# One layer of a streaming encoder: the slots of the split-weight ring get a pitch of 1032 elements

## The chip, the cores and the metric

The kernel runs on one core of one Trainium2 chip. The metric is the time of one execution in microseconds (us), as the median of three runs. The profile is of one further execution, and its times are also in us unless marked ns.

## The reference, cut to what matters

One layer takes `x` (256 tokens by 2048 channels, float32) through a token-mixing half and a feed-forward half:

```python
h = rmsnorm(x, g_pre_mix)
proj = h @ w_in                       # 2048 x (8 groups of 2048 + 16 gates + 2048)
...                                   # mLSTM heads and differential attention on proj
y_m = (sigmoid(m_o) * hm) @ w_branch_m
y_a = ha @ w_branch_a
mix = (g_m * y_m + g_a * y_a) @ w_out
x = x + rmsnorm(mix, g_post_mix)
h = rmsnorm(x, g_pre_ffn)
u = causal_dwconv(h @ w_up)           # 2048 x 11264
y = (gelu(gate) * val) @ w_down       # 5632 x 2048
x = x + rmsnorm(y, g_post_ffn)
```

Nearly all the arithmetic is in the products of a 256-row activation with large float32 weights, and every weight is read from memory once.

## The kernel before

**Split products.** Each float32 operand is split into two float32r parts, `hi` (the rounded value) and `lo` (the rest). A product is then three matmuls into one place in PSUM: hi times hi, hi times lo, lo times hi. The helper `three` (lines 1110 to 1114) issues them in the order of lines 1112, 1113, 1114: stationary hi with moving hi, stationary hi with moving lo, stationary lo with moving hi. Each matmul loads its stationary operand anew.

**The ring of weights.** Weights pass in 648 units of 1024 columns (`UNIT`), 512 KB each, through a ring of `RING = 4` slots. For unit n, SyncE loads `raw[slot]` by DMA; ScalarE writes `w_hi[slot]` as a rounded copy of it (line 517, in `split`); VectorE writes `w_lo[slot] = raw - w_hi` (line 813); TensorE then runs the unit's matmuls and gives the slot back. The splits run three units ahead (`LOOKAHEAD`).

**Stages on TensorE.**
- Gates: 48 matmuls with a small piece of `w_in`, kept in `hm_hi` and `hm_lo`, as the stationary operand and `h` as the moving one.
- Mixer, 4 turns of 64 units. In 6 of 8 chunks the weight is stationary and `h_hi` or `h_lo` is moving (`unit_channels`: 24 matmuls of 256 columns in a unit). In the other 2 chunks `h` is stationary and the weight moves (`unit_tokens`: 12 matmuls of 512 columns). The heads' small matmuls stand between the units.
- Branches, 4 turns of 24 units, all `unit_channels`: 8 units with `h`, 8 with `hm_hi`/`hm_lo`, 8 with `ha_hi`/`ha_lo` as the moving operand.
- Output projection and down projection, 32 and 88 units of `rows_unit` (lines 1278 to 1292): a tile of activations `ks_hi`/`ks_lo` is stationary, the weight moves, 12 matmuls of 512 columns in a unit. The last four units of each use `h_hi` and `h_lo` as room for their split weights.
- Up projection, 176 units of `unit_channels` with `h` moving.

So there are 9600 matmuls with the weight stationary and `h` moving, 1536 with the weight stationary and `hm` or `ha` moving, 768 with `h` stationary, and 1440 in the two row stages.

**What sets the order.** Nothing is scheduled by a program. Every engine runs its own list in the order written, and semaphores tie the lists together.

**Where the tensors lie.** SBUF tensors are laid one behind another in each partition, in the order of the `sb(...)` calls, each start rounded up to 32 bytes: `raw`, `w_hi`, `w_lo`, `h_hi`, `h_lo`, `chan`, `shp`, `stat`, `terms`, `gm`, `hm_hi`, `hm_lo`, `ha_hi`, `ha_lo`, then the heads' tensors; `ks_hi` and `ks_lo` stand further on. `h`, `hm` and `ha` are 16 tiles of 1024 bytes, a slot is 4096 bytes, and each of a slot's stationary tiles of 128 columns is 512 bytes. The built program has these start addresses in a partition, in bytes:

| tensor | before | before, modulo 512 |
|---|---|---|
| `raw` | 16512 | 128 |
| `w_hi` | 32896 | 128 in every slot |
| `w_lo` | 49280 | 128 in every slot |
| `h_hi`, `h_lo` | 65664, 82048 | 128 |
| `hm_hi`, `hm_lo`, `ha_hi`, `ha_lo` | 119872, 136256, 152640, 169024 | 64 |
| `ks_hi`, `ks_lo` | 209984, 214080 | 64 |

Of the kernel before, what the change touches and what calls it, by code (L numbers as in the profile page):

```python
# [40 lines left out]
F32R = mybir.dt.float32r  # L41
# [5 lines left out]
P = 128  # L47
# [20 lines left out]

RING = 4
UNIT = 1024  # L70
LOOKAHEAD = 3
UNITS_CHUNK = KT // 2
TURNS_MIX, U_MIX = 4, 8 * UNITS_CHUNK
# [55 lines left out]
def build_layer(nc, x, w_in, w_branch_m, w_branch_a, w_out, g_post_mix, w_up, w_down, g_post_ffn,  # L129
# [9 lines left out]
    with ctx:  # L139
        def sb(name, shape, dt=F32, stack=ctx):  # L140
            return stack.enter_context(nc.sbuf_tensor(name, shape, dt))
# [3 lines left out]


        raw = sb("raw", [P, RING, UNIT])
        w_hi = sb("w_hi", [P, RING, UNIT], F32R)
        w_lo = sb("w_lo", [P, RING, UNIT], F32R)
        h_hi = sb("h_hi", [P, KT, T], F32R)  # L150
        h_lo = sb("h_lo", [P, KT, T], F32R)
        chan = sb("chan", [P, C_ALL])
# [158 lines left out]

        h_units = [part[:].rearrange("p k t -> p (k t)").rearrange("p (s c) -> p s c", c=UNIT) for part in (h_hi, h_lo)]

# [38 lines left out]
        def _(sp):  # L352
            def load(n, slot, dst_src):
                sp.wait_ge(raw_free, n + 1)
                dst, src = dst_src
                sp.dma_start(dst, src).then_inc(raw_loaded[slot], 16)
# [6 lines left out]
            def rows_loads(turns, per_turn, base, view):  # L363
                for u in range(per_turn):
                    k, half = rows_place(u, True)
                    load(base + u, u % RING, (raw[:, u % RING:u % RING + 1, :],
                                              view[:, k:k + 1, half * UNIT:(half + 1) * UNIT]))
                with sp.Fori(1, turns - 1) as turn:
                    for u in range(per_turn):
                        k, half = rows_place(u, False)  # L370
                        load(turn * per_turn + (base + u), u % RING,
                             (raw[:, u % RING:u % RING + 1, :],
                              view[:, ds(turn * 4 + k, 1), half * UNIT:(half + 1) * UNIT]))
                for u in range(per_turn):
# [140 lines left out]
        def _(scalar):  # L515
# [3 lines left out]
            def split(n4, n, slot):  # L519

                scalar.wait_ge(raw_loaded[slot], n4 * 16 + 16)
                scalar.wait_ge(pe_done, n + 1)
                copy(w_hi[:, slot, :], raw[:, slot, :]).then_inc(hi_done, 1)

            def split_ahead(turn, per_turn, base, u):
                u += LOOKAHEAD
                split(turn * (per_turn // RING) + (base + u) // RING, turn * per_turn + (base + u), u % RING)
# [5 lines left out]
            def norm_tiles(count, gain):  # L533

                for k in range(KT):
                    if k % 2 == 0:
                        scalar.wait_ge(h_psum, (count + k) // 2 + 1)
                    ins = copy(h_hi[:, k, :], ps[:, tile_bank(k), k % 2 * T:k % 2 * T + T],
                               scale=chan[:, gain + k:gain + k + 1])
                    if k % 2:  # L540
                        ins.then_inc(h_hi_done, 1)
# [27 lines left out]
            norm_tiles(0, C_GPM)  # L569
            for u in range(1, LOOKAHEAD):  # L570
                split(0, u, u)
# [117 lines left out]
            def split_last(first_unit, u):  # L689
                n = first_unit + u  # L690
                scalar.wait_ge(raw_loaded[u % RING], n // RING * 16 + 16)
                if u < RING:
                    scalar.wait_ge(pe_done, n + 1)
                copy(last_split(u)[0], raw[:, u % RING, :]).then_inc(hi_done, 1)

            def rows_phase(turns, per_turn, base, src, scale, src_ready, then_load, rest=None):
# [6 lines left out]
                def turn(g, first, last):  # L703
                    for u in range(per_turn):
                        if not last:
                            split_ahead(g, per_turn, base, u)
                        elif u + LOOKAHEAD < per_turn:
                            split_last(g * per_turn + base, u + LOOKAHEAD)
                        if first and u == 5:
# [97 lines left out]
        def _(vec):  # L807
# [3 lines left out]
            def split(n, slot):  # L811
                vec.wait_ge(hi_done, n + 1)
                nc.vector.tensor_tensor(w_lo[:, slot, :], raw[:, slot, :], w_hi[:, slot, :].bitcast(F32),  # L813
                                        ALU.subtract).then_inc(lo_done, 1)

            def split_ahead(turn, per_turn, base, u):
                u += LOOKAHEAD
                split(turn * per_turn + (base + u), u % RING)

            def norm_tiles(count, gain, halfway=None):  # L820
                for k in range(KT):
                    if k == KT // 2 and halfway:
                        halfway()
                    if k % 2 == 0:
                        vec.wait_ge(h_hi_done, (count + k) // 2 + 1)
                    stt(h_lo[:, k, :], ps[:, tile_bank(k), k % 2 * T:k % 2 * T + T], chan[:, gain + k:gain + k + 1],
                        h_hi[:, k, :].bitcast(F32), ALU.mult, ALU.subtract).then_inc(h_done, 1)
# [25 lines left out]
            norm_tiles(0, C_GPM)  # L853
            for u in range(1, LOOKAHEAD):
                split(u, u)
# [518 lines left out]
```

## Time and profile before

| | |
|---|---|
| median of 3 runs | 1934.59 us (1934.44 to 1935.26) |
| the profiled execution's own time | 1934.15 us |
| its span, first to last instruction | 1932.4 us |
| TensorE matmul busy | 1901.5 us, 98% of the span |
| VectorE, ScalarE busy | 1099.8 us (57%), 897.5 us (46%) |
| DMA | 351.35 MB, mean 182 GB/s |

A group's "mean ns of one" for a matmul is its whole pass through the array. Neighbouring matmuls overlap in it, so it is longer than the distance between two starts. What one more matmul costs is that distance, which a list of instructions in order of time shows. TensorE is busy in nearly the whole span, and the granted clock is full in nearly all of it, so the time is close to the sum of these distances.

### The profile page before, as it was taken

To read this page: it belongs to the slowest core of one execution; us is meant where nothing else is said; L and a number is where in the kernel's file an instruction comes from. 1 tells how busy PE (TensorE), PEld (TensorE's weight loads), DVE (VectorE), ACT (ScalarE), POOL (GpSimd) and SP (SyncE) were. 2 spreads that over 40 slices of the span, in tenths; PEclk is the share of its full clock that TensorE was granted. 3 is DMA by queue.
4 is the path that set the end of the run, shared out by engine and by line. 5 is a ranking of instruction groups with operands and counts; after the bars stand their busy time and mean duration, and the time that the engine had idled before them with its cause. 6 is when DMAs were issued, how large, how long until landed. Compare 5 with 4: busy or idle time off the path is not lost.

```text
span 1932.4 us, 35840 instructions
## 1 busy us (share of the span) xinstructions
PE 1901.5 (98%) x13774; PEld 1805.6 (93%) x13774; DVE 1099.8 (57%) x1287; ACT 897.5 (46%) x1159; POOL 74.9 (4%) x103
## 2 busy tenths in 40 slices
PE   6999999999999999999999998999999999999998
PEld 6999999999999999999999888999999999988886
DVE  5555555645655466444554556666666666755545
ACT  5444445444544455443434455454444554544443
POOL 4600000000000000000000000000000000000000
PEclk9999999999999999999999998999999999999999
DMA  6655655566555655565665754666666666565554
GB/s 206 197 174 165 181 172 172 174 175 175 170 179 170 177 166 180 170 191 190 185 191 190 256 177 142 182 183 181 183 184 183 179 182 183 182 214 190 192 189 141
DMA packets 166294, 351.35 MB, mean 182 GB/s; under 512 B 12916, under 2 KB 13517, under 8 KB 165581
## 3 DMA queue, kind: packets, MB, share of 16 engines
q1 hardware_dynamic: 165005, 344.40, 58.5%
q10 hardware_dynamic: 848, 4.79, 0.6%
q0 software_dynamic: 368, 1.09, 0.2%
q8 instruction: 58, 0.95, 0.2%
q14 instruction: 15, 0.12, 0.0%
HBM read 348.12 MB, written 2.12 MB: 181 GB/s over the span
## 4 chain that ended last, share of the span: by engine, by line
issue 59%; PE 39%; SPq 0%; POOLq 0%; DVE 0%; DMA 0%; ACT 0%; POOL 0%; DVEq 0%; ACTq 0%
PE ps L1112 12%; PE ps L1114 12%; PE ps L1113 12%; PE ps L1174 1%; PE ps L1247 1%; PE ps L1224 0%; PE ps L1182 0%; DMA raw<-in_w_in 0%; POOLq L446 0%; PE ps L1223 0%; SPq L387 0%; POOL stat L447 0%; SPq L389 0%; PE ps L1230 0%; SPq L381 0%
## 5 line engine op out<-in xcount | busy, mean ns | idle before, releaser
L813 DVE TENSOR_TENSOR w_lo<-raw,w_hi 128x1024 fp32r<-128x1024 f32 x638 | 781.9, 1229 | 721.4 <-ACT w_hi L517 718.3
L517 ACT ACTIVATE w_hi<-raw 128x1024 fp32r<-128x1024 f32 x640 | 676.3, 1059 | 841.7 <-PE ps L1114 681.8
L1112 PE MATMUL ps<-h_hi,w_hi 128*128 128x256 f32 x3200 | 908.3, 284 | 0.0
L1114 PE MATMUL ps<-h_hi,w_lo 128*128 128x256 f32 x3200 | 905.7, 283 | 0.0
L1113 PE MATMUL ps<-h_lo,w_hi 128*128 128x256 f32 x3200 | 905.7, 283 | 0.0
L1112 PEld LDWEIGHTS ps<-h_hi,w_hi 128*128 128x128 f32 x3200 | 614.5, 192 | 0.5
L1113 PEld LDWEIGHTS ps<-h_lo,w_hi 128*128 128x128 f32 x3200 | 614.5, 192 | 0.5
L1114 PEld LDWEIGHTS ps<-h_hi,w_lo 128*128 128x128 f32 x3200 | 614.3, 192 | 0.0
L1286 PE MATMUL ps<-w_hi,ks_hi 128*128 128x512 f32 x448 | 176.0, 393 | 0.2 <-DVE ks_lo L809 0.2
L1290 PE MATMUL ps<-w_lo,ks_hi 128*128 128x512 f32 x448 | 175.1, 391 | 0.0
L1286 PE MATMUL ps<-w_hi,ks_lo 128*128 128x512 f32 x448 | 138.7, 391 | 0.0
L1286 PEld LDWEIGHTS ps<-w_hi,ks_lo 128*128 128x128 f32 x448 | 84.1, 188 | 19.0
L1286 PEld LDWEIGHTS ps<-w_hi,ks_hi 128*128 128x128 f32 x448 | 84.2, 188 | 18.5 <-issue 0.4
L1290 PEld LDWEIGHTS ps<-w_lo,ks_hi 128*128 128x128 f32 x448 | 84.1, 188 | 18.1
L1112 PE MATMUL ps<-w_hi,h_hi 128*128 128x512 f32 x256 | 100.9, 394 | 0.0
L1113 PE MATMUL ps<-w_lo,h_hi 128*128 128x512 f32 x256 | 99.7, 390 | 0.0
L1114 PE MATMUL ps<-w_hi,h_lo 128*128 128x512 f32 x256 | 99.7, 389 | 0.0
L809 DVE SCALAR_TENSOR_TENSOR xn<-ps,chan,xn 128x254 f32<-128x254 f32 (+1 forms) x176 | 76.6, 477 | 28.4 <-ACT xn L767 21.3
L1112 PE MATMUL ps<-hm_hi,w_hi 128*128 128x256 f32 x256 | 70.7, 276 | 0.0
L1113 PE MATMUL ps<-hm_lo,w_hi 128*128 128x256 f32 x256 | 70.7, 276 | 0.0
L1114 PE MATMUL ps<-hm_hi,w_lo 128*128 128x256 f32 x256 | 70.7, 276 | 0.0
L1112 PE MATMUL ps<-ha_hi,w_hi 128*128 128x256 f32 x256 | 70.7, 276 | 0.0
(166 smaller groups left out, 1381.0 us busy)
## 6 DMA issues: line engine op xcount, KB each, us to landing
raw<-in_w_in SPq DMA_DIRECT2D x288, 512.0 KB, 3.7
raw<-in_w_up SPq DMA_DIRECT2D x176, 512.0 KB, 4.1
raw<-in_w_down SPq DMA_DIRECT2D x88, 512.0 KB, 4.6
raw<-in_w_branch_m SPq DMA_DIRECT2D x32, 512.0 KB, 4.7
raw<-in_w_branch_a SPq DMA_DIRECT2D x32, 512.0 KB, 4.6
raw<-in_w_out SPq DMA_DIRECT2D x32, 512.0 KB, 3.8
x<-in_x ACTq DMA_DIRECT2D x1, 2048.0 KB, 11.6
gm<-in_x SPq DMA_DIRECT2D x3, 512.0 KB, 6.5
```

The lines of the kernel that those rows point to most:

```text
L517: return nc.scalar.activation(out_ap, in_ap, ACT.Copy, scale=scale)
L809: return nc.vector.scalar_tensor_tensor(out=out_ap, in0=in0, scalar=scalar, in1=in1, op0=op0, op1=op1)
L813: nc.vector.tensor_tensor(w_lo[:, slot, :], raw[:, slot, :], w_hi[:, slot, :].bitcast(F32), ALU.subtract).then_inc(lo_done, 1)
L1112: nc.tensor.matmul(out_ap, stat_hi, mov_hi, start=start, stop=False, skip_group_check=True)
L1113: nc.tensor.matmul(out_ap, stat_hi, mov_lo, start=False, stop=False, skip_group_check=True)
L1114: return nc.tensor.matmul(out_ap, stat_lo, mov_hi, start=False, stop=stop, skip_group_check=True)
L1174: last = nc.tensor.matmul(out_ap, weights[:, part * P:(part + 1) * P], v[:, s, j, 0:out_ap.shape[1]], start=i == 0, stop=i == len(parts) - 1)
L1247: last = nc.tensor.matmul(ps[:, 4 + j, (0, 256)[s]:(256, 384)[s]], kT[:, 2 * j + dt, s * P:(s + 1) * P], qT[:, 2 * j + dt, s * P:T], start ...
L1286: ins = nc.tensor.matmul(o, a, hi[:, n * 512:n * 512 + 512], start=first and kslot == 0 and part is ks_hi, stop=last and kslot == 3 and pa ...
L1290: nc.tensor.matmul(o, a, lo[:, n * 512:n * 512 + 512], start=False, stop=False, skip_group_check=True)
```

## The change

`w_hi` and `w_lo` get rows of 1032 elements for each slot, of which the first 1024 are used; a slot is now 4128 bytes behind the one before it. A small unused tensor `w_rest` follows them. Its size works out as 64 elements (256 bytes), so that `h_hi` starts at a whole multiple of 512 bytes behind `w_hi`.

```diff
 RING = 4
 UNIT = 1024
+PITCH = UNIT + 8
 LOOKAHEAD = 3
...
         raw = sb("raw", [P, RING, UNIT])
-        w_hi = sb("w_hi", [P, RING, UNIT], F32R)
-        w_lo = sb("w_lo", [P, RING, UNIT], F32R)
+        w_hi = sb("w_hi", [P, RING, PITCH], F32R)[:, :, 0:UNIT]
+        w_lo = sb("w_lo", [P, RING, PITCH], F32R)[:, :, 0:UNIT]
+        sb("w_rest", [P, 2 * (UNIT - RING * (PITCH - UNIT) % UNIT) % P])
         h_hi = sb("h_hi", [P, KT, T], F32R)
         h_lo = sb("h_lo", [P, KT, T], F32R)
```

Every engine's list of instructions, with their order, shapes and waits, stays the same. Only start addresses change. With s as the slot (0 to 3), they are:

| tensor | after | after, modulo 512 |
|---|---|---|
| `raw` | 16512 | 128 |
| `w_hi` slot s | 32896 + 4128 s | 128 + 32 s |
| `w_lo` slot s | 49408 + 4128 s | 256 + 32 s |
| `h_hi`, `h_lo` | 66176, 82560 | 128 |
| `hm_hi`, `hm_lo`, `ha_hi`, `ha_lo` | 120384, 136768, 153152, 169536 | 64 |
| `ks_hi`, `ks_lo` | 210496, 214592 | 64 |

Everything behind `w_lo` moves by 512 bytes, so it keeps its start modulo 512; the slots of `w_hi` and `w_lo` do not.

## Rows read from the trace of the kernel before

**Rows 1.** The page: busy time of TensorE; its granted clock in 40 slices.

```profile
PE 1901.5 (98%) x13774; PEld 1805.6 (93%) x13774; DVE 1099.8 (57%) x1287; ACT 897.5 (46%) x1159; POOL 74.9 (4%) x103
...
PEclk9999999999999999999999998999999999999999
```

**Rows 2.** Waits of TensorE: total us, times, longest.

```profile
PE ps L1191 <- DMA prob<-in_channel_rows: 13.6, 1, 13.6
PE ps L1148 <- DVE xn L837: 7.8, 1, 7.8
PE ps L1148 <- DVE h_lo L809: 0.8, 1, 0.8
PE ps L1286 <- DVE ks_lo L809: 0.2, 1, 0.2
```

**Rows 3.** Groups by line and shape: count, busy us, mean ns, idle before.

```profile
L1112 PE MATMUL ps<-h_hi,w_hi 128*128 128x256 f32 x3200 | 908.3, 284 | 0.0
...
L1112 PE MATMUL ps<-hm_hi,w_hi 128*128 128x256 f32 x256 | 70.7, 276 | 0.0
...
L1112 PE MATMUL ps<-ha_hi,w_hi 128*128 128x256 f32 x256 | 70.7, 276 | 0.0
```

**Rows 4.** Two stretches of one branch turn: busy us (instructions), granted clock, DMA.

```profile
876.00:894.00 18.00, 18.00 (x152) 18.00 (x151) 7.99 (x7) 7.07 (x7) 0.00 (x0) 1.00 0.56 179
898.00:916.00 18.00, 18.00 (x162) 18.00 (x161) 8.54 (x7) 7.44 (x7) 0.00 (x0) 1.00 0.59 191
```

**Rows 5.** TensorE in order of time, `h` moving: start us, duration us.

```profile
874.80 0.28 PE L1112 MATMUL ps<-h_hi,w_hi 128*128 128x256 f32 x1
...
881.40 0.28 PE L1113 MATMUL ps<-h_lo,w_hi 128*128 128x256 f32 x1
```

**Rows 6.** The same view, `hm` moving.

```profile
899.78 0.28 PE L1112 MATMUL ps<-hm_hi,w_hi 128*128 128x256 f32 x1
...
906.47 0.28 PE L1114 MATMUL ps<-hm_hi,w_lo 128*128 128x256 f32 x1
```

**Rows 7.** The same view, the gates: `hm` stationary, `h` moving.

```profile
21.87 0.28 PE L1113 MATMUL ps<-h_lo,hm_hi 128*128 128x256 f32 x1
...
27.29 0.28 PE L1114 MATMUL ps<-h_hi,hm_lo 128*128 128x256 f32 x1
```

**Rows 8.** The same view, `unit_tokens`: `h` stationary, the weight moving.

```profile
153.55 0.39 PE L1112 MATMUL ps<-w_hi,h_hi 128*128 128x512 f32 x1
...
162.85 0.39 PE L1114 MATMUL ps<-w_hi,h_lo 128*128 128x512 f32 x1
```

**Rows 9.** The same view, down projection: `ks` stationary, the weight moving.

```profile
1705.02 0.39 PE L1290 MATMUL ps<-w_lo,ks_hi 128*128 128x512 f32 x1
...
1715.78 0.39 PE L1286 MATMUL ps<-w_hi,ks_hi 128*128 128x512 f32 x1
```

**Rows 10.** All engines in order of time: matmuls and loads of stationary operands (PEld).

```profile
299.82 0.28 PE L1113 MATMUL ps<-h_lo,w_hi 128*128 128x256 f32 x1
299.82 0.19 PEld L1114 LDWEIGHTS ps<-h_hi,w_lo 128*128 128x128 f32 x1
299.94 0.28 PE L1114 MATMUL ps<-h_hi,w_lo 128*128 128x256 f32 x1
299.94 0.19 PEld L1112 LDWEIGHTS ps<-h_hi,w_hi 128*128 128x128 f32 x1
```

**Rows 11.** The page: the splits on VectorE and ScalarE, as Rows 3.

```profile
L813 DVE TENSOR_TENSOR w_lo<-raw,w_hi 128x1024 fp32r<-128x1024 f32 x638 | 781.9, 1229 | 721.4 <-ACT w_hi L517 718.3
L517 ACT ACTIVATE w_hi<-raw 128x1024 fp32r<-128x1024 f32 x640 | 676.3, 1059 | 841.7 <-PE ps L1114 681.8
```

## The prediction

> **What bounds the kernel now.** I read the page first. TensorE is busy in 98% of the span, and the granted clock reads full (2.4 GHz) in nearly every slice [rows 1]. Next, the waits of TensorE: 13.6, 7.8, 0.8 and 0.2 us [rows 2], all of them at the start or between the two halves. So no buffer, DMA or other engine sets the pace. What sets it is the distance between the starts of two matmuls, taken 13774 times.
>
> Then the groups. The same instruction has a mean of 284 ns with `h` moving and 276 ns with `hm` or `ha` moving [rows 3]. It has the same shape, line and stationary tensor. Two stretches of 18 us inside one branch turn show the same: 152 matmuls with `h`, 162 with `hm`, both at clock 1.00 [rows 4]. For exact distances I divide the time between two far starts by the matmuls between them:
> - `h` moving: 6.60 us over 55 matmuls, 120.0 ns [rows 5].
> - `hm` moving: 6.69 us over 59, 113.4 ns [rows 6].
> - gates, `hm` stationary and `h` moving: 5.42 us over 46, 117.8 ns [rows 7].
> - `unit_tokens`: 9.30 us over 41, 226.8 ns for 512 columns [rows 8].
> - down projection: 10.76 us over 47, 228.9 ns for 512 columns [rows 9].
>
> From 256 to 512 columns at the same distance of operands, 120.0 becomes 226.8 ns, so 256 further columns cost 106.8 ns. That is what 256 columns take at one per cycle of 2.4 GHz (106.7 ns). So 106.7 is the floor of a 256-column matmul, and 120.0 holds 13.3 ns of something else.
>
> What else differs between the first three? Only addresses. The load of the next stationary operand starts with each matmul [rows 10], so two streams read SBUF together: the moving operand of one matmul and the stationary operand of the next. Let d be the stationary start minus the moving start, modulo 512 bytes. Before, d is 0 for the weights against `h` (128 - 128) in every slot, +64 against `hm` and `ha` (128 - 64), and -64 in the gates and the row stages (64 - 128). My reading is that d sets the extra time: 120.0 at 0, 113.4 at +64, 117.8 at -64. Higher address bits seem not to matter. The 9600 `h` matmuls take every slot, every k tile and both odd and even multiples of 512, and rows 3 show one mean for them. The 284 ns there fits the 120.0 ns of rows 5.
>
> This bears on a rule. The Trainium skill's page "TensorE: Matmul & The Clock Gate", section "Step-by-step: what each phase is for", says TensorE has two independent SBUF read ports, and that loading the next weights takes no read bandwidth from the running matmul. "SBUF — State Buffer", section "Who interferes with whom", adds that PE never waits on anyone. By that rule no address could matter and the change would be worth 0. The 120.0 against 113.4 ns of rows 5 and 6 speaks against it; the rule has a rival below.
>
> **The change part by part.** It removes and adds no instruction and moves none in its queue. After it, by the start addresses:
> - Weights against `h`: `w_hi` slot s has d = 32s, which is 0, 32, 64, 96; `w_lo` has d = 128 + 32s, which is 128, 160, 192, 224. In each triple two loads are of `w_hi` and one of `w_lo`, so of the 9600 matmuls each slot has 1600 of the first kind and 800 of the second.
> - Against `hm` and `ha` (1536): `w_hi` 64, 96, 128, 160; `w_lo` 192, 224, 256, 288.
>
> Two classes are known from rows. Slot 0 of `w_hi` keeps d = 0: 1600 matmuls stay at 120.0, worth nothing. Slot 2 of `w_hi` gets d = 64, today's distance of `hm`: 1600 x (113.4 - 120.0) = -10.6 us.
>
> The other 6400 `h` matmuls have distances that no row shows. Bounds: the floor 106.7 from below. From above, the highest extra seen is that of rows 9, 228.9 less 106.7 for the second 256 columns, which is 122.2 ns. I take 117.1, the mean of the three levels seen (120.0, 113.4, 117.8), since no row is nearer to any of these distances than the others. That is 6400 x -2.9 = -18.6 us (bounds -85.1 and +14.1).
>
> The branches: of the 1536, the 256 with `w_hi` in slot 0 (two thirds of a quarter) keep d = 64. The other 1280 go from 113.4 to 117.1: +4.7 us (bounds -8.6 and +11.3).
>
> `unit_tokens` (768) and the row stages (1440): the weight is now the moving operand, and d changes in all but slot 0 of `w_hi`. Rows 8 and 9 show only 226.8 and 228.9 for two different d, so long matmuls look less sensitive. I take 0. Bounds: down to twice the floor, 213.4, which is 768 x 13.4 + 1440 x 15.5, some -33 us; and up by the 2.1 ns between these rows, +5 us.
>
> The splits: VectorE and ScalarE now write slots at other offsets, off the critical path either way. A channel unit on TensorE is 24 x 120.0 = 2.88 us, against 1.23 and 1.06 us for its two splits, and VectorE idles 718.3 us waiting for ScalarE, which idles 681.8 us waiting for TensorE [rows 11]. At 24 x 113.4 = 2.72 us a unit they stay hidden. `raw` doesn't move, so the DMAs are the same. The 512 bytes by which all other tensors move leave their starts modulo 512 as they are. The float32 matmuls of the heads have no `w` in them: 0.
>
> Sum: -10.6 - 18.6 + 4.7 + 0 = -24.5 us. On the profiled execution's 1934.15 us (span 1932.4 and 1.75 around it) that is 1909.7, and the median is 0.44 above that execution, so 1910 us. The gain can't be given back by a wait: nothing else is near TensorE's pace.
>
> **The rivals.**
> *The unknown distances are nearly free.* Then 6400 matmuls sit between the floor and 113.4, say at 110.0: -64.0 - 10.6 - 1280 x 3.4 = -79 us, 1856 us. For it: d = 0 looks like the most crowded case, with both streams at the same offset, and a move by 64 took half of the extra away. Against: -64 took away only 2.2 of 13.3 ns, so a move alone doesn't free it.
>
> *The distance isn't what counts.* Either the two reads don't meet at all, or the moving operand's own start decides (`hm` starts at 64 modulo 128, `h` at 128, before and after). Both give 0: 1934.6 us. The first is what the two pages of the Trainium skill named above say. For the second: it explains rows 5 against 6. Against: the gates move the same `h` as the branches and take 117.8 instead of 120.0 [rows 5, 7], with only the stationary operand's place changed.
>
> *The unknown distances are worse.* A larger distance could make the two streams meet more often, not less: within a matmul they sweep 1024 and 512 bytes, so d only says where they begin. The place is every channel unit, slots 1 and 3 and all `w_lo`. At the upper bound of 122.2 ns the cost is 6400 x 2.2 = +14.1, and the branches, which stand at the best level known, lose 1280 x 8.8 = +11.3; with -10.6 that is +15 us, 1949 us. It decides when the mean of the unknown distances passes 120.2 ns: there -10.6 + 6400 x 0.2 + 1280 x 6.8 is about 0. For it: the long matmuls at -64 are slower than at 0 [rows 8, 9]. Against: of three short levels none is above 120.0.
>
> **How the numbers follow.** Forecast 0.60, nearly free 0.13, no effect 0.11, worse 0.16. A change within 0.2% (3.9 us) can't be told from none. So faster 0.73, same 0.11, slower 0.16. The forecast's own range is 1885 to 1928, the unknown mean level between 114 and 119.5 with a few us for the long matmuls. For 8 in 10 I reach down to 1868, which leaves out most of the nearly free case, and up to 1944, which takes in no effect and the milder half of worse.
>
> **What the profile after would show.** By slot, channel units of `h`: slot 2's `w_hi` intervals at 113.4, slot 0's at 120.0, and the two must differ between slots that before were alike. If slot 2 stays at 120.0, the distance modulo 512 is the wrong variable. The `hm` and `ha` stretches should lose their even 113.4. TensorE's waits should stay at 22 us and the clock full; a new wait of TensorE for `w_lo` would make the covered splits wrong. If the mean over the 6400 is outside 114 to 119.5, the step that failed is the value taken for the unknown distances.

## The result, and the profile after

| | before | after |
|---|---|---|
| median of 4 runs on one chip | 1934.92 us | 1924.64 us |
| ratio | | 0.9947, 95% interval 0.9934 to 0.9959 |
| span of the profiled execution | 1932.4 us | 1922.5 us |

The change makes the kernel 10 us faster. The direction and the place were right; the size forecast, -24.5 us, was 2.4 times the measured one.

Lines of the changed kernel are two higher than before (1112 is 1114). These are its groups by line and shape: count, busy us, mean ns, idle before. They answer to [rows 3].

```profile
L1114 PE MATMUL ps<-h_hi,w_hi 128*128 128x256 f32 x3200 | 899.7, 281 | 0.0
...
L1288 PE MATMUL ps<-w_hi,ks_hi 128*128 128x512 f32 x448 | 176.3, 394 | 0.0
...
L1114 PE MATMUL ps<-w_hi,h_hi 128*128 128x512 f32 x256 | 101.9, 398 | 0.0
...
L1115 PE MATMUL ps<-hm_lo,w_hi 128*128 128x256 f32 x256 | 71.9, 281 | 0.0
```

The mean with `h` moving fell from 284 to 281 ns and the one with `hm` rose from 276 to 281 (line 1115; its line before, 1113, stood at 276 as well). The waits of TensorE (us in total, times, longest) are what they were, but for one at the start that grew from 0.8 to 2.1 us in this execution; the one of 0.2 us is gone:

```profile
PE ps L1193 <- DMA prob<-in_channel_rows: 13.6, 1, 13.6
PE ps L1150 <- DVE xn L839: 7.8, 1, 7.8
PE ps L1150 <- DVE h_lo L811: 2.1, 1, 2.1
```

Two stretches of the changed kernel, inside `h` and inside `hm` units of one branch turn. As in [rows 4], a line has the stretch and its length, then the busy us and the instructions (x) of TensorE's matmuls, of its loads, of VectorE, ScalarE and GpSimd, then the granted clock, the DMA share and GB/s:

```profile
876.00:894.00 18.00, 18.00 (x156) 18.00 (x155) 7.36 (x7) 8.34 (x8) 0.00 (x0) 1.00 0.58 187
898.00:914.00 16.00, 16.00 (x138) 16.00 (x137) 7.27 (x7) 6.37 (x6) 0.00 (x0) 1.00 0.60 188
```

With `h`, 18 us now hold 156 matmuls instead of 152. With `hm`, 16 us hold 138; the old rate of 113.4 ns puts 143 there (141, and the two that reach over the edges).

The long matmuls became slower too. The same 40 us of the down projection, before and after, hold 177 and 175:

```profile
1690.00:1730.00 40.00, 40.00 (x177) 32.81 (x176) 21.74 (x24) 18.04 (x23) 0.00 (x0) 1.00 0.66 220
1690.00:1730.00 40.00, 40.00 (x175) 32.49 (x174) 19.98 (x23) 18.37 (x23) 0.00 (x0) 1.00 0.59 202
```

I took the distance between neighbouring starts for every matmul of both traces and summed it by kind (differences are taken before rounding):

| kind | before, us | after, us | difference | predicted |
|---|---|---|---|---|
| 9600 with `h` moving | 1154.9 | 1130.5 | -24.4 | -29.2 |
| 1536 with `hm` or `ha` moving | 174.5 | 181.1 | +6.6 | +4.7 |
| 768 of `unit_tokens` | 175.7 | 179.0 | +3.4 | 0 |
| 1440 of the row stages | 329.9 | 333.0 | +3.0 | 0 |
| all else | 97.3 | 98.9 | +1.5 | 0 |
| span | 1932.4 | 1922.5 | -9.9 | -24.5 |

By slot, in the up projection, where 176 units run without a break, 44 of each slot:

| slot | distance of `w_hi`, `w_lo` from `h` | before, ns | after, ns |
|---|---|---|---|
| 0 | 0, 128 | 120.0 | 119.3 |
| 1 | 32, 160 | 120.0 | 117.9 |
| 2 | 64, 192 | 120.0 | 114.8 |
| 3 | 96, 224 | 120.1 | 117.8 |

So the distance from start to start does depend on where the weights lie. The writes of the splits into the same memory are not what it depends on. In the up projection before, the mean distance is 120.0 ns for the matmuls during which VectorE was writing a `w_lo` (some 1600) and 120.0 for the others (some 2600); after, it is 117.4 and 117.5.

### The profile page after: what moved, and what is told of

Same layout as the page of the kernel before. It is cut to its first block, busy times and chain, and to the rows that moved or that the text cites. A ratio compares the mean times of both kernels' runs of the same rounds, so it can differ in the third digit from the quotient of the medians.

```text
span 1922.5 us, 35840 instructions
## 1 busy us (share of the span) xinstructions
PE 1890.7 (98%) x13774; PEld 1788.4 (93%) x13774; DVE 1099.3 (57%) x1287; ACT 898.7 (47%) x1159; POOL 75.4 (4%) x103
## 4 chain that ended last, share of the span: by engine, by line
issue 59%; PE 39%; SPq 0%; POOLq 0%; DMA 0%; DVE 0%; ACT 0%; POOL 0%; DVEq 0%; ACTq 0%
PE ps L1116 12%; PE ps L1114 12%; PE ps L1115 12%; PE ps L1176 1%; PE ps L1249 1%; PE ps L1226 0%; PE ps L1184 0%; DMA raw<-in_w_in 0%; POOLq L448 0%; PE ps L1225 0%; SPq L389 0%; POOL stat L449 0%; PE ps L1150 0%; PE ps L1232 0%; SPq L383 0%
## 5 line engine op out<-in xcount | busy, mean ns | idle before, releaser
L1115 PE MATMUL ps<-h_lo,w_hi 128*128 128x256 f32 x3200 | 896.3, 280 | 0.0
L1116 PE MATMUL ps<-h_hi,w_lo 128*128 128x256 f32 x3200 | 895.2, 280 | 0.0
L1115 PEld LDWEIGHTS ps<-h_lo,w_hi 128*128 128x128 f32 x3200 | 603.9, 189 | 0.6
L1116 PEld LDWEIGHTS ps<-h_hi,w_lo 128*128 128x128 f32 x3200 | 602.9, 188 | 0.0
L1114 PEld LDWEIGHTS ps<-h_hi,w_hi 128*128 128x128 f32 x3200 | 602.2, 188 | 0.6
L1115 PE MATMUL ps<-ha_lo,w_hi 128*128 128x256 f32 x256 | 71.9, 281 | 0.0
L1116 PE MATMUL ps<-ha_hi,w_lo 128*128 128x256 f32 x256 | 71.8, 280 | 0.0
```

The costliest lines, as they stand in the source:

```text
L1114: nc.tensor.matmul(out_ap, stat_hi, mov_hi, start=start, stop=False, skip_group_check=True)
L1115: nc.tensor.matmul(out_ap, stat_hi, mov_lo, start=False, stop=False, skip_group_check=True)
L1116: return nc.tensor.matmul(out_ap, stat_lo, mov_hi, start=False, stop=stop, skip_group_check=True)
```

## The experiments

The padded kernels below add unused SBUF only; all do the same arithmetic. "Distance" is stationary start minus moving start modulo 512 bytes, as in the prediction. The times of e3, e4, e10 and e11 are single runs.

### e1_d64 and e8_d64_again: all weights at 64

```diff
+        sb("pad_h", [P, 112])
         h_hi = sb("h_hi", [P, KT, T], F32R)
         h_lo = sb("h_lo", [P, KT, T], F32R)
+        sb("pad_chan", [P, 16])
         chan = sb("chan", [P, C_ALL])
```

> Before, with 448 unused bytes ahead of h_hi and 64 behind h_lo: every weight tile stands at +64 modulo 512 from h, hm and ha; nothing else changes modulo 512. Distance theory (stationary start minus moving start, modulo 512, sets the extra time): all 9600 matmuls with h moving take 113.4 ns instead of 120.0, -63 us; unit_tokens goes from distance 0 to -64 and so from 226.8 to about 229, +2 us; 1874 us. The gates go from -64 to 0, 117.8 to 120.0. Rival 'no contention': 1935 us. Rival 'the moving operand's own start modulo 128': h now starts at 64 as hm does, so it also gives 113.4; the next kernel tells these two apart.

Measured: 1894.77 us, ratio 0.9791 (0.9775 to 0.9807). That is 20 us short of the theory, and one of the five runs took 1912.69 us. The mean with `h` moving was 117.2 ns in its trace, and `hm` and `ha`, whose distance I hadn't touched, had gone from 113.4 to 117.8. One distance, two levels: so the prediction's premise, one level for each distance, fell here. The same kernel again:

> The kernel with h, hm and ha all at 64, once more. Its five runs were 1893.96, 1894.60, 1894.77, 1894.84 and 1912.69 us, and the last is the one profiled, with its 4224 matmuls of the up projection at 117.7 ns. Theory of two levels: 4224 x 4.4 ns = 18.6 us is the whole gap, so the other runs had 113.3 in the up projection; the times of this kernel fall into separate clusters about 19 us apart (or sums of such steps for the other stages), none in between. A profile of a run near 1894 would show the up projection at 113.3 ns. Rival (some other disturbance in one run): all runs near 1894, and their profile has 117.7 in the up projection just the same.

Measured: 1893.98, 1894.07, 1895.05, 1895.86, 1895.99 and 1913.08 us. Two clusters again, and this time the profiled run was one near 1894. The same stretch of the up projection in both executions, first the one of 1912.69 us:

```profile
1200.00:1240.00 40.00, 40.00 (x342) 40.00 (x342) 25.77 (x32) 19.78 (x24) 0.00 (x0) 1.00 0.61 182
1400.00:1440.00 40.00, 40.00 (x342) 40.00 (x342) 26.47 (x31) 20.45 (x24) 0.00 (x0) 1.00 0.64 187
```

and the one of 1894.07 us:

```profile
1200.00:1240.00 40.00, 40.00 (x355) 40.00 (x355) 27.44 (x34) 19.64 (x24) 0.00 (x0) 1.00 0.61 193
1400.00:1440.00 40.00, 40.00 (x356) 40.00 (x355) 28.18 (x35) 21.27 (x25) 0.00 (x0) 1.00 0.59 188
```

The program and the granted clock (1.00) are the same, yet 40 us hold 342 matmuls or 355. A stretch also counts the two or three that reach over its edges; without them it is 117.8 and 113.3 ns. Once in a level the stream stays in it for all 176 units; in the mixer the level changes only where the heads' small matmuls or long matmuls come between. 4224 x 4.5 ns = 19 us is the gap between the clusters. (One execution of each cluster was profiled.)

Two smaller predictions of e1 held, in both traces: the gates, now at 0, went from 117.8 to 120.0 ns, and `unit_tokens`, now at -64, took 1.5 us more (+2 expected).

### e2_all_moved: every tensor 64 bytes further on

```diff
+        sb("pad_raw", [P, 16])
         raw = sb("raw", [P, RING, UNIT])
```

> Before, with 64 unused bytes ahead of raw: every tensor starts 64 bytes further on, all distances between them are the same. Distance theory: every interval as before (120.0 with h moving, 113.4 with hm), 1935 us. Rival 'the moving operand's own start modulo 128 decides': h now starts at 64 modulo 128 and hm at 0, so h falls to 113.4 and hm rises to 120.0: 9600 x -6.6 + 1536 x 6.6 = -53 us, 1882 us.

Measured: 1934.86 us, ratio 1.0002 (0.9993 to 1.0012). The stretch that answers to the first of [rows 4]:

```profile
876.00:894.00 18.00, 18.00 (x152) 18.00 (x152) 9.46 (x9) 6.50 (x7) 0.00 (x0) 1.00 0.62 188
```

The same 152. A shift of everything by 64 bytes changes nothing, so the rival of the moving operand's own start is out: what counts is relative.

### e5_pitch_only and e6_lo128_only: the two parts of the change apart

```diff
-        w_hi = sb("w_hi", [P, RING, UNIT], F32R)
-        w_lo = sb("w_lo", [P, RING, UNIT], F32R)
+        w_hi = sb("w_hi", [P, RING, PITCH], F32R)[:, :, 0:UNIT]
+        sb("pad_lo", [P, 96])
+        w_lo = sb("w_lo", [P, RING, PITCH], F32R)[:, :, 0:UNIT]
+        sb("pad_h", [P, 96])
```

> The change without the 128-byte offset of w_lo: slots of w_hi and w_lo both stand at 0, 32, 64, 96 from h. Levels of the changed kernel by slot are 119.6, 118.0, 114.8, 117.9 ns. If the pitch makes the change's time, this kernel has the same levels and 1923 to 1927 us. Rival: the offset of w_lo (128) makes it, then this one is near 1935.

```diff
         w_hi = sb("w_hi", [P, RING, UNIT], F32R)
+        sb("pad_lo", [P, 32])
         w_lo = sb("w_lo", [P, RING, UNIT], F32R)
+        sb("pad_h", [P, 96])
```

> The change without the pitch: all slots of w_hi at 0 from h, all of w_lo at 128; against hm 64 and 192. If the pitch makes the change's time, h stays at the 119.6 ns of the changed kernel's slot 0 and hm near 114: 1930 to 1936 us. Rival (w_lo's offset makes it): 1923 to 1927 us.

Measured: pitch alone 1933.72 us, ratio 0.9998 (0.9989 to 1.0007); offset alone 1933.35 us, 0.9995 (0.9986 to 1.0004). Neither is a measurable gain, and together they give 10 us. I had expected the pitch to carry it; that was wrong. By slot in the up projection, pitch alone has 119.9, 118.2, 117.9 and 117.4 ns, offset alone 119.1 in all. What pitch alone lacks is slot 2, 117.9 instead of 114.8. Its -16.2 us on `h` are eaten by +7.4 us on `hm` and `ha`, +3.4 us on `unit_tokens` and +5.0 us on the row stages. Offset alone leaves `hm` and `ha` (here at 64 and 192) at 113.3, but its -8.5 us on `h` are eaten by +6.6 us on the long matmuls. On `h` the two gains simply add up (-24.7, against -24.4 together). What makes the whole worth more than its parts is the losses: each part alone pays for the long matmuls (+8.4 and +6.6), and both together pay once (+6.4).

Pitch alone also shows 64 with 64 in two ways of coming in. In its up projection slot 2, behind slot 1 at 32, stays at 117.9 in all 44 units. In its branches slot 0 has the same 64 with 64, behind slot 3 at 96 or 160, and falls to 113.3 after some four matmuls in all 16 units.

### e12_slot2_lo64: one address of the changed kernel

The slots are cut by hand from one long row; the offsets in elements are those of the changed kernel except slot 2 of `w_lo` (and a place for slot 3 that has the same start modulo 512).

```diff
+HI_OFF = (0, 8, 16, 24)
+LO_OFF = (0, 8, 112, 152)
...
+        w_hi = Ring(sb("w_hi", [P, RING * UNIT + 32], F32R), HI_OFF)
+        w_lo = Ring(sb("w_lo", [P, RING * UNIT + 152], F32R), LO_OFF)
+        sb("pad_h", [P, 72])
```

> The changed kernel with one address changed modulo 512: w_lo of slot 2 at 64 from h instead of 192 (and at 128 instead of 256 from hm and ha). Theory: slot 2 no longer gets to 113.3 and goes from 114.8 to 118, 2400 x 3.0 = +7 us over the changed kernel, 1930 to 1933 us. Rival (slot 2 is fast because w_hi is at 64): slot 2 stays near 115, 1923 to 1926 us.

Measured: 1931.15 us, ratio 0.9981 (0.9972 to 0.9991). Slot 2 is at 118.0 ns, the others at 118.9, 117.9 and 117.9. A slot 2 unit of the changed kernel, with its 24 matmuls from 1281.29 on, in order of time (start, duration):

```profile
1281.29 0.28 PE L1114 MATMUL ps<-h_hi,w_hi 128*128 128x256 f32 x1
...
1282.00 0.28 PE L1114 MATMUL ps<-h_hi,w_hi 128*128 128x256 f32 x1
...
1283.93 0.28 PE L1116 MATMUL ps<-h_hi,w_lo 128*128 128x256 f32 x1
```

The same unit with `w_lo` at 64:

```profile
1284.37 0.28 PE L1125 MATMUL ps<-h_hi,w_hi 128*128 128x256 f32 x1
...
1285.08 0.28 PE L1125 MATMUL ps<-h_hi,w_hi 128*128 128x256 f32 x1
...
1287.08 0.28 PE L1127 MATMUL ps<-h_hi,w_lo 128*128 128x256 f32 x1
```

Both begin with 0.71 us for six matmuls, 118 ns each. Then the changed kernel takes 1.93 us for 17, 113.5 each; with the one address moved it is 2.00 us, 117.6 each. So slot 2 of the changed kernel isn't fast because `w_hi` is at 64 alone, but because `w_hi` at 64 together with `w_lo` at 192 pulls the stream into the low level within six matmuls. Once there, the loads of `w_hi` and of `w_lo` cost the same: all three lines stand at 113.4.

### e9_hi64_lo192: that pair in every slot

```diff
         w_hi = sb("w_hi", [P, RING, UNIT], F32R)
+        sb("pad_lo", [P, 32])
         w_lo = sb("w_lo", [P, RING, UNIT], F32R)
+        sb("pad_h", [P, 80])
         h_hi = sb("h_hi", [P, KT, T], F32R)
         h_lo = sb("h_lo", [P, KT, T], F32R)
+        sb("pad_chan", [P, 16])
```

> In the changed kernel slot 2 has w_hi at 64 and w_lo at 192 from h, and falls to 113.3 ns within its first 6 matmuls even out of slot 1's 118; with both at 64 (pitch alone) slot 2 stays at 118. Theory: the pair 64/192 has only the low level, or pulls the stream to it; the pair 64/64 holds either. Here all slots have 64/192 against h, hm and ha. Theory: 113.3 in every channel stage of every run: 9600 x -6.7 = -64 us, hm and ha 0, long matmuls (at -64 and -192) +4 to +8: 1875 to 1882 us, and all runs in one cluster. Rival (each pair holds either level, by chance of entry): some stages at 117.7, 1890 to 1920 us, runs in separate clusters.

Measured: 1876.93 us, ratio 0.9704 (0.9691 to 0.9717), all five runs within 1876.20 to 1878.56. It beats before by 58 us and the change by 48 (the kernel before stood at 1934.89 us beside it, and at 1934.92 beside the change). The up projection, twice, and an `hm` stretch ahead of it:

```profile
842.00:856.00 14.00, 14.00 (x126) 14.00 (x125) 8.48 (x7) 5.42 (x6) 0.00 (x0) 1.00 0.61 187
1200.00:1240.00 40.00, 40.00 (x355) 40.00 (x354) 26.55 (x34) 21.27 (x25) 0.00 (x0) 1.00 0.67 198
1400.00:1440.00 40.00, 40.00 (x355) 40.00 (x355) 27.32 (x35) 20.46 (x25) 0.00 (x0) 1.00 0.65 191
```

Again 355 in 40 us, and 126 in 14 us with `hm` (113.3 ns each): 9600 matmuls with `h` took 1091.9 us (-63.0), `hm` and `ha` 174.5 (the same as before), and the long ones together +5.6 us.

The Trainium skill's rule of two independent read ports ("TensorE: Matmul & The Clock Gate", "Step-by-step: what each phase is for") says that the load of the next weights takes no read bandwidth from the running matmul. The traces do not agree: three unused gaps in SBUF change the time by 58 us, with the same instructions and clock. There may be two ports, which no run here shows. But for these float32r streams the load is not free, and the measurement decides.

### e3, e4, e7, e10, e11: other distances

> w_hi stands at +64 from h, w_lo at 0. Which stationary read meets which moving read? If the matmul runs beside the load of the NEXT stationary operand, the distance from the start of line 1112's and line 1114's matmul to the next start is 113.4 ns and that of line 1113 (w_lo is loaded next) is 120.0. If it meets its own load, lines 1112 and 1113 are at 113.4 and line 1114 (w_lo its own) at 120.0. Either way two thirds of -63 us and one third of hm's 1536 matmuls worse by 6.6: about 1934.6 - 42 + 3.4 + 2 = 1898 us. If instead one bad load spoils its neighbours, all three lie between.

> Weights stand at -64 from h (h moved by 64 bytes), so unit_tokens has +64; ks stands at +64 from the weights instead of -64. Distance theory with the gates' level for -64: 117.8 ns with h moving, 9600 x -2.2 = -21 us. Rival 'only the distance modulo 128 counts' (-64 and +64 are then the same): 113.4 ns, -63 us. For the long matmuls at +64 the trace of before has no level; if the sign matters as it does for the short ones they fall below 226.8 and 228.9, if it is modulo 128 the row stages stay at 228.9. The gates, here at -128, stay near 120.0 if modulo 128 counts.

> Theory of two levels: at distance 64 the stream of matmuls holds either 113.3 or 117.7 ns for as long as nothing disturbs it, and which one is set by how it comes in; coming from distance 0 it falls to 113.3, as hm after h in the kernel before. Here slot 0 stands at 0 and slots 1 to 3 at 64 from h, hm and ha, so each fourth unit comes from 0. Theory: slot 0 at 120.0, the others at 113.3 to 114.5 in every stage and every run: 9600 x -4.7 = -45, hm and ha +3, long matmuls 0 to +5, so 1893 to 1898 us, and no run apart from the rest. Rival (one level for each distance, which the run of the d64 kernel put at 117.2 on the mean): slots 1 to 3 at 117.2, 1918 us or more.

> w_hi at 64 as there, w_lo at 320. If any w_lo that is apart from w_hi by more than the 64/64 case will do, h is at 113.3 too, about 1880 us. If 192 (which is 64 modulo 128) is what counts, 320 (64 modulo 128 as well, one period of 256 further) gives the same; a level of 117.7 or a mix, 1905 to 1920 us, would say that the half period of 128 between w_hi and w_lo matters by itself.

> All slots as the changed kernel's slot 1: w_hi at 32, w_lo at 160 from h, 64 and 192 from hm and ha. If 118.0 is the own level of this pair, h is at 118.0 throughout: 9600 x -2.0 = -19, long matmuls +6, about 1922 us. Rival: slot 1's 118.0 in the changed kernel is a mean of what the neighbours leave behind, and the pair's own level is something else (113 to 120).

The edits are gaps ahead of `w_lo`, `h_hi`, `chan` and `ks_hi`, in elements:

```diff
 e3:  +sb("pad_lo", [P, 112])                          +sb("pad_chan", [P, 16])
 e4:  +sb("pad_h", [P, 16])   +sb("pad_chan", [P, 112]) +sb("pad_ks", [P, 32], stack=branch)
 e7:  slot offsets (0, 16, 16, 16) for w_hi and w_lo, +112 ahead of w_lo and h_hi, +16 ahead of chan
 e10: +sb("pad_lo", [P, 64])  +sb("pad_h", [P, 48])     +sb("pad_chan", [P, 16])
 e11: +sb("pad_lo", [P, 32])  +sb("pad_h", [P, 88])     +sb("pad_chan", [P, 8])
```

| kernel | distance from `h`: hi, lo | time, us | `h` in the up projection, ns | `hm`, `ha`: distance, ns |
|---|---|---|---|---|
| e3 | 64, 0 | 1929.89 | 117.8 | 64, 0: 117.8 |
| e4 | -64, -64 | 1931.64 | 117.8 | 64, 64: 117.8 |
| e7 | slot 0 at 0, others 64 | 1926.28 (4 runs) | 119.9; 117.8 to 118.0 | the same: 120.0; 117.8 |
| e10 | 64, 320 | 1893.94 | 113.3 | 64, 320: 117.8 |
| e11 | 32, 160 | 1927.52 | 118.9 | 64, 192: 113.3 |

- e3 failed to tell which load meets which matmul: all three lines stand at 117.6 to 118.6, none at 113.4 or 120.0. No unit of it is at 113.3. Whether `w_lo` at 0 keeps it from there isn't shown, since 64 with 64 can hold 117.8 too.
- e4 has 117.8, as the gates had. Six units in its mixer show 113.3, so -64 has both levels too. `ks` at +64 made the row stages 5.8 us longer, and `h` at +64 made `unit_tokens` 4.6 us longer, though every slot and both parts have one distance. The stretch of the down projection shown above for before and after, in e4:

```profile
1690.00:1730.00 40.00, 40.00 (x173) 32.22 (x172) 20.28 (x24) 18.32 (x24) 0.00 (x0) 1.00 0.63 215
```

- e7 was a miss. I had said that coming from distance 0 leads to the low level, since `hm` after `h` in the kernel before does that. Slots 1 to 3, after slot 0 at 120.0, went to 117.8 nearly everywhere, and the time was 30 us over the expectation. Coming from 0 isn't what selects the low level.
- e10 has e8's level in every channel unit but three of the first mixer turn: `h` 1106.7 against 1107.0 us, the branches 181.2 in both, the long ones 507.1 in both. 320 acts as 64, not as 192. So for `w_lo` the distance counts modulo 256, and the 128 between `w_hi` and `w_lo` does its own work. The up projection in e10, as in e8:

```profile
1200.00:1240.00 40.00, 40.00 (x355) 40.00 (x355) 27.37 (x35) 19.78 (x24) 0.00 (x0) 1.00 0.65 191
```

- e11: slot 1's pair, alone, has 118.9 ns in the up projection and 117.9 to 118.7 in the mixer, so it too has more than one level; among its neighbours slot 1 has 117.9. Its branches, at 64 and 192, are at 113.3, coming in from 118.9.

## Why the prediction was wrong in its size

- **What bounds the kernel**: right. The time moved with the distance between matmul starts and, for 1.5 us, with the start of the kernel. No new wait came, the clock stayed as it was but for some 3 us at the start, and the covered splits stayed covered. (The wait of 0.2 us in [rows 2] stands at 1072.7 us, ahead of the output projection, and not at the start or between the halves; nothing hangs on it.)
- **The relative start of the stationary and the moving operand matters, the absolute one does not**: right, by e1 and e2. That it is their two reads that collide is inferred; the traces show starts of instructions, not reads.
- **One level for each distance**: wrong, and the worst error in the reasoning. At 64 the same program holds 117.8 or 113.3 ns (e1, e8). The 113.4 that [rows 6] gave for 64 was one of the two. With it falls the sum's way of pricing each load by its own distance, `w_hi` apart from `w_lo`: in slot 2 both stand at 113.4 once the stream is there.
- **Slot 0 stays, slot 2 goes to 113.4**: the numbers came out near (the sum's own terms give 119.0 and 114.6 with `w_lo` in them, measured were 119.3 and 114.8), but for slot 2 by luck. Without `w_lo` at 192 it would have been 118.0 (e12).
- **117.1 ns for the 6400 of unknown distance**: too low by 0.7 to 0.8 ns. Slots 1 and 3 came to 117.9 and 117.8. This, slot 0 and some of slot 2 are the 4.8 us between -29.2 and -24.4. The same value for the branches was too low too: inside the units of their slots 1 to 3 it was 117.9, 118.2 and 120.7, +6.6 against +4.7. So a distance can also be worse than 0, which no row before had shown.
- **0 for the long matmuls**: the term that was mis-sized most. They grew by 3.4 and 3.0 us, 6.4 together. The reasoning was that two distances with nearly one level (226.8 and 228.9) meant they hardly react. The runs show that they do: pitch alone +8.4 us, offset alone +6.6, and in e4, where every slot and both parts have one distance of +64, +10.4. The 0 and -64 of before happened to be the two best distances seen for them.
- The rest is +1.5 us. The one wait at the start is 1.3 longer, and behind it the granted clock reads 0.50 (1.2 GHz) from 21.0 to 22.5 us, where it read 1.00 before, so that the first gates' matmuls start 214 ns apart and not 118. This is one pair of executions.

These misses, 4.8 + 1.9 + 6.4 + 1.5 = 14.6 us, are the distance from -24.5 to -9.9 us. The rival "worse" was right about one of the losses: the branches stood at their best level and lost it. Its condition, a mean of the unknown distances above 120.2 ns, did not come, and it did not have the long matmuls.

What stays open: why 64 with 192 was at the low level in every stage and run where all slots had it; what selects between the two levels at 64 with 64; which load meets which matmul, for which e3 was meant; and which of the two reads gives way. The traces give start times, not the single reads.

## What to carry to other kernels

If TensorE is busy throughout and the starts of equal matmuls are further apart for one operand tensor than for another, look at the addresses of the stationary and the moving operand relative to each other before looking at any engine. Padding costs a few hundred bytes in each partition, and one uniform relation chosen by measurement (here 64 and 192 bytes) was worth 3%, where a different relation in each slot was worth 0.5%. Do not read a level off one place in a trace as the property of an address: see that it holds in several runs and after several ways in, and try the parts of a layout together, since here two parts worth nothing measurable each gave 10 us.

## What the runs showed of the hardware

- With float32r operands, 128 stationary columns and 256 moving columns, the distance between starts held steady at 120.0, 117.8 or 113.3 ns at the relative starts 0, 64 and -64, at full clock. Others lay between (118.9 at 32 with 160, 119.1 at 0 with 128) or, with `w_hi` at 160 and `w_lo` at 288 from `hm` in the changed kernel, above (120.7). The best is still 6.6 ns over the 106.7 that 256 columns take at one per cycle of 2.4 GHz.
- With 512 moving columns it was 226.8 to 229 ns at 0 and -64, and 233 at +64 (e4).
- For `w_lo` the relation has a period of 256 bytes (e10 against e8).
- Writes of VectorE and ScalarE into the weights' slots did not change a steady level: 120.0 ns with and without them before, 113.3 with and without them in e8 and e9.
- The stream of matmuls has two steady states at one layout, and can stay in either for 4224 matmuls. This makes a program's times fall in two clusters 19 us apart, at the same granted clock: of 11 runs of e1 and e8, 2 were in the longer one.
